# Four standing columns for the modulation products of two conditioning vectors

## What is computed

```
silu_c = silu(c);  silu_cc = silu(c_ctx)
mod   = silu_c  @ ada_w[i] + ada_b[i]          # 1024 -> 6144
mod_c = silu_cc @ ada_w[i] + ada_b[i]
sh_m, sc_m, g_m, sh_f, sc_f, g_f = split(mod, 6)     # the same for mod_c
h = modulate(rmsnorm(x, norm_mix_w[i]), sh_m, sc_m)  # shift and scale
x = x + g_m * mixer(h)                               # gate
x = x + g_f * swiglu(modulate(rmsnorm(x, ...), sh_f, sc_f), ...)
```

## Time and profile before

| what | us |
|---|---|
| median of three runs | 4288.87 |
| the profiled execution, its own time | 4293.29 |
| its span, first to last instruction | 4291.4 |
| PE busy | 3625.2 (84%) |
| DVE busy | 1872.6 (44%) |
| ACT busy | 1217.3 (28%) |
| mean granted TensorE clock | 0.911 of full speed |

### The profile page before, as it was taken

The page is one execution under the profiler, slowest core; times in us unless marked ns, Lnnn a source line. Parts: engine busy times, 40 slices in busy tenths (PEclk is TensorE's granted clock), DMA queues, the critical chain, the costliest instruction groups (busy, mean ns, idle before and its releaser), DMA issues. The chain is left out here.

```text
span 4291.4 us, 40160 instructions
## 1 busy us (share of the span) xinstructions
PE 3625.2 (84%) x16676; PEld 2873.9 (67%) x16676; DVE 1872.6 (44%) x2533; ACT 1217.3 (28%) x1650; POOL 172.6 (4%) x128
## 2 busy tenths in 40 slices
PE   7776687899896797899879787899998894668998
PEld 6464576787783676787648566788784473547876
DVE  2447444444425444444461464321245526654234
ACT  3110333323324433323451242211224311013223
POOL 0013000000000000000000000000000003520000
PEclk9885798999998898999999899999999996779999
DMA  4110131232220131232452201122115320012332
GB/s 136 44 59 0 40 118 30 82 96 85 94 90 30 40 118 30 81 96 84 153 181 69 45 1 59 50 61 68 60 65 181 119 76 0 1 40 79 98 94 79
DMA packets 326679, 314.40 MB, mean 73 GB/s; under 512 B 22289, under 2 KB 249873, under 8 KB 326105
## 3 DMA queue, kind: packets, MB, share of 16 engines
q1 hardware_dynamic: 326496, 311.82, 23.3%
HBM read 309.58 MB, written 2.22 MB: 73 GB/s over the span
## 5 line engine op out<-in xcount | busy, mean ns | idle before, releaser
L284 PE MATMUL ps<-hT_hi,w_hi 128*128 128x512 f32 (+1 forms) x2640 | 968.2, 367 | 25.1 <-DVE arena L824 11.0
L285 PE MATMUL ps<-hT_lo,w_hi 128*128 128x512 f32 (+1 forms) x2640 | 966.3, 366 | 0.0
L286 PE MATMUL ps<-hT_hi,w_lo 128*128 128x512 f32 (+1 forms) x2640 | 965.3, 366 | 0.0
L249 DVE TENSOR_TENSOR w_lo<-raw,w_hi 128x1024 fp32r<-128x1024 f32 (+2 forms) x510 | 591.2, 1201 | 666.4 <-ACT w_hi L239 666.3
L284 PE MATMUL ps<-w_hi,hT_hi 128*128 128x512 f32 (+1 forms) x1768 | 703.9, 398 | 123.6 <-DVE hT_lo L721 77.7
L285 PE MATMUL ps<-w_lo,hT_hi 128*128 128x512 f32 (+1 forms) x1768 | 701.3, 397 | 0.0
L286 PE MATMUL ps<-w_hi,hT_lo 128*128 128x512 f32 (+1 forms) x1768 | 699.6, 396 | 0.0
L239 ACT CAST w_hi<-raw 128x1024 fp32r<-128x1024 f32 (+2 forms) x510 | 501.2, 1033 | 544.0 <-PE ps L286 531.4
L284 PEld LDWEIGHTS ps<-hT_hi,w_hi 128*128 128x128 f32 x2640 | 499.4, 189 | 112.0 <-issue 22.4
L286 PEld LDWEIGHTS ps<-hT_hi,w_lo 128*128 128x128 f32 x2640 | 499.0, 189 | 81.4
L285 PEld LDWEIGHTS ps<-hT_lo,w_hi 128*128 128x128 f32 x2640 | 499.4, 189 | 80.3
(11 more groups left out here) (236 smaller groups left out, 3076.9 us busy)
## 6 DMA issues: line engine op xcount, KB each, us to landing
raw<-in_ffn_w_in SPq DMA_DIRECT2D x88, 512.0 KB, 4.7
raw<-in_ada_w SPq DMA_DIRECT2D x24, 1024.0 KB, 5.2
arena<-in_ada_w SPq DMA_DIRECT2D x24, 1024.0 KB, 5.6
raw<-in_ffn_w_gate SPq DMA_DIRECT2D x44, 512.0 KB, 4.0
raw<-in_ffn_w_up SPq DMA_DIRECT2D x44, 512.0 KB, 5.3
raw<-in_ffn_w_out SPq DMA_DIRECT2D x20, 1024.0 KB, 5.0
raw<-in_ffn_w_down SPq DMA_DIRECT2D x20, 1024.0 KB, 5.1
raw<-in_ev_w_in SPq DMA_DIRECT2D x16, 1024.0 KB, 5.6
```

The lines of the kernel that those rows point to most:

```text
L249: ins = dve.tensor_tensor(lo[:, half], self.raw_chunk(c)[:, half], hi[:, half].bitcast(F32), ALU.subtract)
L284: pe.matmul(out, w[0], x[0], start=first, stop=False)
L285: pe.matmul(out, w[0], x[1], start=False, stop=False)
L286: return pe.matmul(out, w[1], x[0], start=False, stop=last)
```

## The change

The high and low parts of both vectors now stand together as four columns (c high, c_ctx high, c low, c_ctx low). Each tile of a chunk is multiplied by two products, the four columns by the high part of the weights and by the low part. The result has four rows, of which the first and third belong to c, the second and fourth to c_ctx; they are added only at the end, by a product with a small matrix `fold` (4x2, two unit matrices one above the other). For the shifts and scales this product takes the place of the 48 transposes. For the gates four further products of 512 columns give the two rows, ACT copies them out, and SP stores them alone. The bias must be added once, so its rows 2 and 3 are cleared, by a memset of 4x6144 on DVE ahead of the bias load, for which SP waits.

```diff
--- before.py
+++ after.py
@@ -119,7 +119,7 @@
              ("ffn_g0", 8), ("ffn_g1", 8), ("ret_g", 4), ("hg_g", 4), ("lb", 12), ("odq", 1), ("odk", 1),
              ("xaq0", 2), ("xaq1", 2), ("xak0", 2), ("xak1", 2), ("cw0", 66), ("cw1", 66), ("cb0", 22),
              ("cb1", 22), ("nm0", 8), ("nm1", 8), ("nf0", 8), ("nf1", 8), ("c", 8), ("cc", 8),
-             ("sgun", 4), ("decb", 4), ("ghn", 1)]
+             ("sgun", 4), ("decb", 4), ("ghn", 1), ("fold", 2)]
     plan, at = {}, 0
     for name, n in names:
         plan[name] = (at, n)
@@ -1461,14 +1461,17 @@
 
 def modulation(k, W, l):
 
-
     A = Arena(k)
-    rows, bias = A(6 * D), A(6 * D)
+    rows, bias, gates = A(6 * D), A(6 * D), A(2 * D)
     sc = A(KD, 2)
     first = W[f"ada{l}"]
     n, nk = 6 * D // BANK, KD // KQ
-    pair = [x[:, :, 0:2] for x in (k.hi, k.lo)]
-    s_c_hi, s_c_lo, s_silu, s_bias, s_side, s_mm_done, s_freed, s_turned, s_modT, s_stored = stage_sems(k, f"ada{l}", "act:c_hi", "dve:c_lo", "act:silu", "dma:bias", "dma:side", "pe:mm_done", "dve:freed", "pe:turned", "dve:modT", "dma:stored")
+    quad = k.hi[:, :, 0:4]
+    fold = k.col("fold", 0, 2)[0:4]
+    gate_chunks = [4, 5, 10, 11]
+    s_c_hi, s_c_lo, s_silu, s_bias, s_side, s_mm_done, s_freed, s_turned, s_folded, s_modT, s_gates, s_clear, s_stored = stage_sems(
+        k, f"ada{l}", "act:c_hi", "dve:c_lo", "act:silu", "dma:bias", "dma:side", "pe:mm_done", "dve:freed", "pe:turned",
+        "pe:folded", "dve:modT", "act:gates", "dve:clear", "dma:stored")
     block = k.block
     for i in range(n * nk):
         k.chunk_used[first + i] = s_mm_done(i + 1)
@@ -1477,14 +1480,17 @@
     def _(sp):
         k.join(sp, "pe", "dve", "act", "pool")
         b = k.ins["ada_b_2"]
+        sp.wait_ge(*s_clear(1))
         sp.dma_start(bias[0:2, :], bass.AP(b.tensor, b.offset + l * 6 * D, [[0, 2], [1, 6 * D]])).then_inc(*s_bias.up(16))
         if l == 0:
             sp.dma_start(k.X[:, TX:TALL, :], k.ins["ctx_2"][0].rearrange("(t p) d -> p t d", p=P)).then_inc(*s_side.up(16))
         k.stream(sp, first + n * nk)
-        sp.wait_ge(*s_freed(n))
-        sp.dma_start(k.mod_rows, rows[0:2, :]).then_inc(*s_stored.up(16))
-        k.loading(s_stored(16))
-        sp.wait_ge(*s_stored(16))
+        sp.wait_ge(*s_gates(4))
+        for i in range(2):
+            sp.dma_start(k.mod_rows[:, (2 + 3 * i) * D:(3 + 3 * i) * D],
+                         gates[0:2, i * D:(i + 1) * D]).then_inc(*s_stored.up(16))
+        k.loading(s_stored(32))
+        sp.wait_ge(*s_stored(32))
         if l == 0:
             k.loading(s_side(16))
 
@@ -1494,9 +1500,12 @@
         for i, name in enumerate(("c", "cc")):
             act.activation(sc[:, :, i], k.col(name, 0, 8), ACT.Silu).then_inc(*s_silu.up(1))
         act.wait_ge(*s_silu(2))
-        act.copy(pair[0], sc).then_inc(*s_c_hi.up(1))
+        act.copy(quad[:, :, 0:2], sc).then_inc(*s_c_hi.up(1))
         for i in range(n * nk + 1):
             k.hi_until(act, first + i + 1)
+        for i in range(4):
+            act.wait_ge(*s_folded(i + 1))
+            act.copy(gates[0:2, i * BANK:(i + 1) * BANK], k.ps[0:2, (5, 6, 7, 3)[i], :]).then_inc(*s_gates.up(1))
 
     @block.tensor
     def _(pe):
@@ -1509,26 +1518,32 @@
                 k.wait_split(pe, first + nk * g + q)
                 w = k.split_chunk(first + nk * g + q)
                 for kk in range(KQ):
-                    ins = split_products(pe, k.ps[0:2, g % 4, :], [x[:, q * KQ + kk, :] for x in pair],
-                                         [x[:, kk, :] for x in w], q == 0 and kk == 0,
-                                         q == nk - 1 and kk == KQ - 1)
+                    c4 = quad[:, q * KQ + kk, :]
+                    pe.matmul(k.ps[0:4, g % 4, :], c4, w[0][:, kk, :], start=q == 0 and kk == 0, stop=False)
+                    ins = pe.matmul(k.ps[0:4, g % 4, :], c4, w[1][:, kk, :], start=False,
+                                    stop=q == nk - 1 and kk == KQ - 1)
                 ins.then_inc(*s_mm_done.up(1))
         pe.wait_ge(*s_freed(n))
+        for i, c in enumerate(gate_chunks):
+            pe.matmul(k.ps[0:2, (5, 6, 7, 3)[i], :], fold, rows[0:4, c * BANK:(c + 1) * BANK], start=True,
+                      stop=True).then_inc(*s_folded.up(1))
         for i in range(48):
-            ins = pe.transpose(k.ps[:, 4, 2 * i:2 * i + 2], rows[0:2, i * P:(i + 1) * P], k.ident[0:2, 0:2])
+            ins = pe.matmul(k.ps[:, 4, 2 * i:2 * i + 2], rows[0:4, i * P:(i + 1) * P], fold, start=True, stop=True)
         ins.then_inc(*s_turned.up(1))
 
     @block.vector
     def _(dve):
+        k.join(dve, "pe", "dve", "act", "pool")
+        dve.memset(bias[0:4, :], 0.0).then_inc(*s_clear.up(1))
         dve.wait_ge(*s_c_hi(1))
-        dve.tensor_tensor(pair[1], sc, pair[0].bitcast(F32), ALU.subtract).then_inc(*s_c_lo.up(1))
+        dve.tensor_tensor(quad[:, :, 2:4], sc, quad[:, :, 0:2].bitcast(F32), ALU.subtract).then_inc(*s_c_lo.up(1))
         k.lo_until(dve, first + 2)
         dve.wait_ge(*s_bias(16))
         for g in range(n):
             k.lo_until(dve, first + min(nk * g + 4, nk * n + 1))
             dve.wait_ge(*s_mm_done(nk * (g + 1)))
-            dve.tensor_tensor(rows[0:2, g * BANK:(g + 1) * BANK], k.ps[0:2, g % 4, :],
-                              bias[0:2, g * BANK:(g + 1) * BANK], ALU.add).then_inc(*s_freed.up(1))
+            dve.tensor_tensor(rows[0:4, g * BANK:(g + 1) * BANK], k.ps[0:4, g % 4, :],
+                              bias[0:4, g * BANK:(g + 1) * BANK], ALU.add).then_inc(*s_freed.up(1))
         dve.wait_ge(*s_turned(1))
         dve.tensor_copy(k.modT[:].rearrange("p a b -> p (a b)"), k.ps[:, 4, 0:96]).then_inc(*s_modT.up(1))
         dve.wait_ge(*s_modT(1))
@@ -2012,6 +2027,7 @@
                           ("cw", "ffn_conv_w"), ("cb", "ffn_conv_b"), ("nm", "norm_mix_w_2"),
                           ("nf", "norm_ffn_w_2")):
             src[f"{name}{l}"] = inputs[key][l]
+    src["fold"] = np.tile(np.eye(2, dtype=np.float32), (P // 2, 1)).T
     plan, n = column_plan()
     return np.concatenate([col(np.asarray(src[name])) for name in plan], 1)
```

## The result

The changed kernel takes **4330.63 us**, the median of five runs (4325.11 to 4331.82), against 4288.87 (4287.87 to 4295.92, five runs) for the kernel before: ratio of the runs **1.0092**, 95% interval 1.0077 to 1.0107 (the two medians alone give 1.0097). The forecast was 4314.0 with a range of 4299 to 4321: the sign is right, the size is not: +41.8 us between the medians where +25.2 were forecast. The profiled execution took 4325.11 us, its span is 4323.3.

What follows compares the result with a forecast made beforehand. No one engine was full; a ring of waits among PE, ACT and DVE held the chunk loop. Per layer +5.2 - 10.1 + 3.4 + 14.1 = +12.6 us, for two +25.2: median 4288.9 to 4314.0 us, range 4299 to 4321.

Steps and rivals of the forecast that it cites:

- The ring: Chunk loop, PE to ACT to DVE to PE: rounds shrink from 6.60 to 5.68 us, -10.1 us per layer.
- The start: Stage beginning: SP's first DMA and the chunks queued behind it wait for the bias memset, +5.2 us per layer.
- 6144 columns come to ... 5.2 us: Memset's price at the stage start, from two memsets: 2.62 us plus 3072 columns at 0.83 ns.
- The tail: Stage end behind the last chunk: fold for the gates +3.4 us and 48 small products +14.1 us per layer.
- So full clock lasts some 3.5 us after the tiny work begins: Small products in the tail: 31 of 96 instructions at full clock, 65 at half, together 17.3 us.
- 3.4 us, at full clock: Fold for the gates, ahead of the small products: eight instructions of 0.43 us each, +3.4 us per layer.
- Both upper ends: Tail at half clock throughout: the fold 6.9 us, the 96 small instructions 20.4 us.
- the forecast's 17.3 us: Time of the 48 small products in each layer's tail, against 3.2 us for the transposes: +14.1 us.
- A (the clock holds): Rival, 0.18: ordinary products in the tail keep full clock, +7.6 us instead of +14.1 per layer, 4301.1 us.
- B (cheap instructions): Rival, 0.10: small products cost 65 ns per instruction, +3.0 us per layer, no slowdown, 4291.9 us.
- C (the fall in the loop): Rival, 0.06: pauses in the chunk loop drop the clock to half, rounds 7.1 us, 15 us more per layer, 4344.

Runs made afterwards that it cites:

- experiment 2: Kernel before with only a bias memset half as wide (4x3072) on DVE and SP's wait for it: 4296.47 us, ratio 1.0013.
- experiment 8: Changed kernel with fold and 48 small products reading all 128 partitions, rows 4 to 127 zeros cleared by POOL: 4324.83 us, ratio 1.0082.
- experiment 10: Changed kernel with eight unused 128-row products ahead of the fold and one more before every fourth small product: 4347.48 us, ratio 1.0126.
- experiment 5: Kernel before with 48 ordinary fp32 products of 2 rows in place of its 48 transposes, nothing else: 4328.89 us, ratio 1.0089.
- experiment 6: Changed kernel with 48 transposes of four rows in place of the 48 small products, DVE adding the pairs: 4302.55 us, ratio 1.0032.
- experiment 9: Changed kernel with its four fold products issued behind the 48 small ones instead of ahead: 4337.04 us, ratio 1.0109.
- experiment 4: Kernel before with the two-product loop alone (low columns left out) and eight unused 128-row products ahead of the transposes: 4278.19 us, ratio 0.9970.
- experiment 7: Changed kernel with eight unused 128-row products of 512 columns between the last chunk and the fold: 4329.84 us, ratio 1.0090.
- the second kernel of 13: Kernel of experiment 13 with six unused 128-row products ahead of the transposes: 4279.83 us, ratio 0.9975.
- the second kernel of 12: Kernel of experiment 12 with ten unused 128-row products between the last chunk and the transposes: 4294.16 us, ratio 1.0013.
- experiment 12: Two-product loop with low columns in 32 and 33 of 34, no fold or memset, transposes of the kernel before, POOL adding the bias: 4293.42 us, ratio 1.0010.
- experiment 13: Kernel of experiment 12 with DVE's taking out one chunk later and the next stage's first low part behind the last group: 4281.42 us, ratio 0.9982.

## Why the forecast was wrong, step by step

**The ring** was right: rounds of 5.6 to 5.7 us, limited as described, DVE full but for 0.46 us, the DMAs no hindrance. Only the first round was longer, at half clock, 1 us per layer off the forecast on average. From 2133 to 2189 the DMAs of the profile after moved 367 GB/s, above the 358 GB/s that the Trainium skill (DMA: Bandwidth & Descriptors, Specifications) gives; the measurement decides.

**The start** was mis-sized: "6144 columns come to ... 5.2 us" is the length of a record. In its place stand 6.65 us (6.4 of them 6144 columns at 1.04 ns, experiment 2), of which 0.7 did not reach ACT's cast of chunk 2. That is 0.8 us per layer more than forecast.

**The tail** is the step that failed: 23.6 and 22.1 us more than before where +17.5 were forecast, 10.7 of the 14 us by which the two stages miss their +25.2. It failed in two sentences. One is "So full clock lasts some 3.5 us after the tiny work begins". I counted from the first tiny instruction. But the fall goes rather by the last wide product (128 rows, 512 columns): in the 30 tails of 15 profiles (all but experiments 8 and 10) it came 2.5 to 5.7 us after the start of that product (before 5.5 and 5.1, after 3.2 and 4.7, the memset alone 2.5 and 2.6). Counted from the first instruction of the fold or the turning it is 0.2 to 5.2 us in the same tails. In the kernel before, the transposes began 1.8 us after it in layer 0, so that 3.7 were left. The changed kernel puts a pause of 2.4 us and then the fold into that time, and nothing was left for the small products: 0 of 96 at full clock instead of 31. That is 20.6 us instead of 17.3.

The other is the fold's "3.4 us, at full clock". It inherits the same clock: 6.2 and 4.6 us. Both upper ends stood in the text, 6.9 and 20.4; with them the tail is 27.3, and the measured 26.9 and 25.4 are just below. But the range took in only the 20.4: its top of 4321 has the small products at half clock from their first and the fold ahead of them at full clock. With 6.9 for the fold the same sum gives 4327.

Experiment 5 shows that the forecast's 17.3 us hold in one layer where small products follow the loop directly, and experiments 6, 8 and 9 that the fold's four rows leave the clock down. For the pause as a cause stand experiments 4, 7 and the second kernel of 13: filled, the transposes or the fold got full clock in all six tails. Against it stands the second kernel of 12, where they did not, in either layer. Why the fall came at 2.5 us in one execution and at 5.7 in another is open; so is how much 128-row work among small products would hold the clock, since experiment 10 tried one dose.

**The rivals.** A (the clock holds) and B (cheap instructions) are refuted by experiment 5 and the changed kernel itself, C (the fall in the loop) by rounds of 5.67 us at a clock of 1.00, the first one excepted; in experiment 12 it happened. The right case was one I had not written down: the forecast's mechanism with its origin two steps earlier. What spoke for A, that only transposes let the clock fall, could have been tested on a row of the kernel before that the prediction leaves out: in the stage behind layer 1's turning PE did nothing but transposes of 128x128 (L521), and the clock rose. Windows of the kernel before:
```profile
3367.80:3371.20 3.40, 3.40 (x17) 3.40 (x18) 2.01 (x4) 0.93 (x2) 0.00 (x0) 0.50 0.00 0
3371.20:3374.60 3.40, 2.32 (x19) 1.84 (x17) 3.18 (x6) 1.07 (x3) 0.00 (x0) 1.00 0.00 0
```

**Part by part.** Alone, the loop gives -9.5 us, the memset +21 (of which some 3 are the turning's clock), the 48 products +37; the change with transposes in their place is at +13. Products cost 28 us in the change itself. These medians do not add up to the change's +42: together the three make +49, without a fold. In the profiles the stages differ by -17.2, +15.5 and +31.7 us, and these with the fold's 10.8 come near the change's 39.3.

## What to carry to other kernels

Where a piece of work ends a stage, look in the trace for the last wide, full-height product ahead of it and for the clock's fall behind that, not from the piece's own beginning, and put everything that now stands between them (pauses, products of few rows) into that time; a tail of small products is best costed at half clock, and shortened by taking the work into the loop or to an idle engine. Where one upper end of a range holds for a piece, ask whether it holds for the piece ahead of it too. An fp32 product that moves 2 columns past 128 standing ones costs two instructions of 0.112 us (0.213 at half clock); a transpose of the same piece takes 0.065 (0.104). The price of a memset was its record and the idle time ahead of it: look ahead of the row that a price is taken from.

## What the runs showed of the hardware that was not expected

- Products that read 4 rows and move 512 columns, without pauses, left the granted clock at half (5.20 of 5.20 us busy); with 128 rows the clock rose to full within the fold (2203.2). The Trainium skill (TensorE: Matmul & The Clock Gate, Part 4) says that transposes do not count as PE work for the clock. The windows of the kernel before shown above do not agree: from 3367.6 PE did nothing but transposes of 128x128, and at 3371.2 the clock rose to 1.00. The measurement decides. Transposes of 2 rows, ordinary products of 2 or 4 rows, and small products of 128 rows and 2 columns were all followed by a fall.
- A memset's record is shorter than the time it takes: 5.18 us recorded, while SP's DMA came 6.65 us later than before; 2.62 and 3.45 for half the columns.
- POOL's addition of 2x512 beside DVE's subtractions: in experiment 13 a pair of subtractions took 2.89 us instead of 2.34, and the addition 2.65. It can go either way, as a round of experiment 12 shows, where the addition took 1.28 us and the pair 3.45 (timeline of its first kernel):
```profile
2150.60 3.45 DVE L249 TENSOR_TENSOR w_lo<-arena,w_hi 128x1024 fp32r<-128x1024 f32 x2
2151.68 1.28 POOL L1516 TENSOR_TENSOR arena<-arena 2x512 f32<-2x512 f32 x1 [4.76 <-ACT arena L1508]
```
  What the addition takes with no subtraction beside it, no run shows. The Trainium skill (GPSIMD Engine Reference, Specifications) says that POOL shares its SBUF interfaces with VectorE, with contention where DVE has two SBUF inputs; the trace agrees.
